# A hybrid decoder step: gate weights divided at another place of the state-space chunk, and zeroes of the expert buffer written in another stage

## The reference, cut to what matters

```
u = xn @ w_in
q, k, v, z, xbc, dt_raw, g_a, g_s = jnp.split(u, offs, axis=-1)
...
y_ssd, new_conv, new_ssm = _ssd_branch(z, xbc, dt_raw, ...)      # a scan over chunks of 128 tokens
merged = (jax.nn.sigmoid(g_a + b_gate[0]) * (y_attn @ w_attn_br)
          + jax.nn.sigmoid(g_s + b_gate[1]) * (y_ssd @ w_ssd_br))
h = x + merged @ w_out
...
h = h + _hier_moe(hn, ...)      # 32 experts, two per token
```

## Time and profile before

| what | number |
|---|---|
| median of 3 runs | 2184.7 us (2180.73 to 2187.69) |
| the profiled execution | 2187.37 us |
| its span | 2185.5 us |
| PE busy | 1899.6 us (87%) |
| DVE busy | 1201.7 us (55%) |
| ACT busy | 818.8 us (37%) |
| POOL busy | 390.8 us (18%) |
| DMA moved | 472.97 MB, mean 216 GB/s |
| prompt state space | about 850 to 1100 us of the span |
| merge | about 1166 to 1340 us of the span |

### The profile page before, as it was taken

The page is one execution under the profiler, slowest core; times in us unless marked ns, Lnnn a source line. Parts: engine busy times, 40 slices in busy tenths (PEclk is TensorE's granted clock), DMA queues, the critical chain, the costliest instruction groups (busy, mean ns, idle before and its releaser), DMA issues. The chain is left out here.

```text
span 2185.5 us, 29251 instructions
## 1 busy us (share of the span) xinstructions
PE 1899.6 (87%) x11737; PEld 1686.6 (77%) x11737; DVE 1201.7 (55%) x1224; ACT 818.8 (37%) x1173; POOL 390.8 (18%) x377
## 2 busy tenths in 40 slices
PE   7999999979986998888883897994899999999970
PEld 7899999978885987777652897883788888888850
DVE  5244443235654221555643554426888888888856
ACT  5211111123341321222232321213677777777732
POOL 0000000055523302011240000001831111111103
PEclk9999999989986999999986998996999999999985
DMA  6355555444427866233229434325999999999957
GB/s 227 128 166 166 166 166 166 143 148 138 127 81 190 212 169 201 92 114 104 80 70 321 141 104 133 128 85 207 351 420 407 407 406 402 402 408 406 401 211 261
DMA packets 203113, 472.97 MB, mean 216 GB/s; under 512 B 34519, under 2 KB 160887, under 8 KB 189922
## 3 DMA queue, kind: packets, MB, share of 16 engines
q1 hardware_dynamic: 134946, 319.29, 41.2%
q10 hardware_dynamic: 51440, 78.21, 9.8%
q0 software_dynamic: 16592, 73.60, 9.8%
HBM read 376.12 MB, written 121.93 MB: 228 GB/s over the span
## 5 line engine op out<-in xcount | busy, mean ns | idle before, releaser
L2736 DVE TENSOR_TENSOR k_w_lo<-expert_raw,k_w_hi 128x4096 fp32r<-128x4096 f32 x96 | 424.2, 4421 | 70.9 <-ACT k_w_hi L2680 70.9
L2680 ACT CAST k_w_hi<-expert_raw 128x4096 fp32r<-128x4096 f32 x96 | 348.4, 3633 | 107.2 <-PE k_pu L74 66.1
L72 PE MATMUL a_acc<-a_w_hi,x_hi 128*128 128x256 f32 x648 | 186.2, 287 | 0.3 <-DVE x_lo L229 0.3
L73 PE MATMUL a_acc<-a_w_lo,x_hi 128*128 128x256 f32 x648 | 184.3, 284 | 0.0
L74 PE MATMUL a_acc<-a_w_hi,x_lo 128*128 128x256 f32 x648 | 184.3, 284 | 0.0
L72 PEld LDWEIGHTS a_acc<-a_w_hi,x_hi 128*128 128x128 f32 x648 | 125.3, 193 | 0.7 <-DVE x_lo L229 0.5
L73 PEld LDWEIGHTS a_acc<-a_w_lo,x_hi 128*128 128x128 f32 x648 | 125.3, 193 | 0.0
L74 PEld LDWEIGHTS a_acc<-a_w_hi,x_lo 128*128 128x128 f32 x648 | 125.2, 193 | 0.0
L72 PE MATMUL k_pu<-k_w_hi,k_x_hi 128*128 128x512 f32 x256 | 105.0, 410 | 9.0 <-DVE k_w_lo L2736 9.0
L72 PE MATMUL k_po<-k_w_hi,k_h_hi 128*128 128x512 f32 x256 | 102.5, 400 | 10.6 <-DVE k_h_lo L2757 10.6
L72 PE MATMUL k_pg<-k_w_hi,k_x_hi 128*128 128x512 f32 x256 | 102.0, 399 | 2.7 <-DVE k_x_lo L2741 2.7
(11 more groups left out here) (458 smaller groups left out, 4853.3 us busy)
## 6 DMA issues: line engine op xcount, KB each, us to landing
expert_raw<-in_w_expert_gate SPq DMA_DIRECT2D x32, 2048.0 KB, 10.7
expert_raw<-in_w_expert_up SPq DMA_DIRECT2D x32, 2048.0 KB, 12.2
expert_raw<-in_w_expert_down SPq DMA_DIRECT2D x32, 2048.0 KB, 11.7
h<-in_cache_kv_w SPq DMA_DIRECT2D x72, 256.0 KB, 4.2
scratch_o_moe<-k_out ACTq DMA_DIRECT2D x32, 512.0 KB, 11.4
a_w<-in_w_in SPq DMA_DIRECT2D x15, 1024.0 KB, 7.2
scratch_u_tm<-h ACTq DMA_DIRECT2D x81, 128.0 KB, 2.1
scratch_o_moe<-h_zeros POOLq DMA_DIRECT2D x2, 4096.0 KB, 29.7
```

The source lines that it names most:

```text
L72: nc.tensor.matmul(out, one_pass(a_hi), one_pass(b_hi), start=(i == 0), stop=False)
L73: nc.tensor.matmul(out, one_pass(a_hi), one_pass(b_lo), start=False, stop=False)
L2680: nc.scalar.copy(one_pass(w_hi[:, kind, :]), raw[:, c % NRAW, :]).then_inc(s_hi, 1)
L2736: nc.vector.tensor_tensor(one_pass(w_lo[:, kind, :]), raw[:, c % NRAW, :], w_hi[:, kind, :], ALU.subtract).then_inc(s_lo, 1)
```

## The change

The division of tile n + 2 moves from the end of chunk n to between the second and the third weighing of chunk n. The zeroes for the unused expert rows are no longer written in the merge (two DMAs of 4,096 KB from a tile of 512 columns) but in the prompt state space: a tile of 256 columns of zeroes is filled at its start, and in each of the eight chunks POOL issues one DMA, behind its gating, that writes half of the 16 row blocks in a quarter of the columns. At the end of the stage POOL waits for all eight.

```
@@ phase_ssd_prompt
+        zeros, s_zeros, s_unused = sb("zeros", [128, 256]), sm("zeros"), sm("unused")
...
                 nc.gpsimd.memset(whole[:, :], 1.0)
+                nc.gpsimd.memset(zeros[:, :], 0.0).then_inc(s_zeros, 1)
                 nc.gpsimd.memset(hT[:, :], 0.0)
...
                     if n > 0:
                         gate(n - 1)
+                    if n == 0:
+                        pool.wait_ge(s_zeros, 1)
+                    a, b = n % 4, n // 4
+                    pool.dma_start(T["o_moe"][(NE + 8 * b) * 128:(NE + 8 * b + 8) * 128, a * 256:(a + 1) * 256].rearrange(
+                        "(b p) c -> p b c", p=128), bc(zeros[:, :].unsqueeze(1), [128, NOVF // 2, 256])).then_inc(s_unused, 16)
                 gate(N - 1)
+                pool.wait_ge(s_unused, 16 * N)
                 pool.wait_ge(s_h0, 16 * NB)
...
                     for q in range(NQ):
                         weigh(n, q)
+                        if q == 1:
+                            gates.split(dve, n + 2)
                     state(n, 0)
...
                     dve.sem_inc(s_free, 1)
-                    gates.split(dve, n + 2)
@@ phase_merge
-        zeros = sb("zeros", [128, 512])
...
-        s_const, s_eps, s_zeros, s_unused = sm("const"), sm("eps"), sm("zeros"), sm("unused")
+        s_const, s_eps = sm("const"), sm("eps")
...
                 nc.gpsimd.memset(T["m_T"][:, :, REAL:], 0.0)
-                nc.gpsimd.memset(zeros[:, :], 0.0).then_inc(s_zeros, 1)
-                pool.wait_ge(s_zeros, 1)
-                for a in range(D // 512):
-                    pool.dma_start(T["o_moe"][NE * 128:, a * 512:(a + 1) * 512].rearrange("(b p) c -> p b c", p=128),
-                                   bc(zeros[:, :].unsqueeze(1), [128, NOVF, 512])).then_inc(s_unused, 16)
-                pool.wait_ge(s_unused, 16 * (D // 512))
```

## The result

The changed kernel takes 2155.53 us (median of 4 runs, 2152.91 to 2158.01) against 2185.2 for the kernel before, a ratio of 0.9861 with an interval of 0.9849 to 0.9874: 30 us less. The forecast was 2154.

| stretch | before, us | after, us | difference |
|---|---|---|---|
| start to prompt state space | 849.97 | 847.65 | -2.3 |
| prompt state space: start to chunk 1 | 47.94 | 48.19 | +0.3 |
| chunks 1 to 6 | 173.45 | 150.54 | -22.9 |
| chunk 7 and end | 28.92 | 30.68 | +1.8 |
| sample state space | 66.12 | 67.32 | +1.2 |

A forecast was written before the change was run, and what follows sets the result against it. PE's order was taken to set the state space's length, its idle time being what can be won. 20.8 + 11.2 = 32.0 us off 2187.37 gives 2155.4, or 2152.7 from the median; forecast 2154, range 2147 to 2167.

The forecast's parts named there:

- Part 1, the division: Prompt state space, chunks 1 to 6: six PE waits for gate weights go, gaining 20.8 us (bounds 17.2 and 20.8).
- The low clock: Chunks 1 to 6: PE's low-clock stretches follow its waits and go with them, 3.6 of the 20.8 us.
- C: Cast's start in chunk 4; inputs end by C + 6.2, division C + 9.6, weighings C + 11 to 12, cost 0.
- The rule weighed against it: DVE and POOL lock their shared ports per instruction; the division pays POOL's gating at most once, sum staying 2155.4 us.
- Chunk 0: Prompt state space, chunk 0: division of tile 2 costs 0, up to 2.5 us if zeroes slow its weights.
- Part 2, the merge: Merge's start: without 8.4 MB of zeroes there, the second rows land earlier, gaining 11.2 us (bounds 7 and 13).
- The 10.7 for the first megabyte of weights: Merge's start: weights ahead of the rows take 16.8 us to land, 6.1 alone, so 10.7 us go.
- The 1.2 for the rows: Merge's start: the rows' own transfer, sharing DMA engines with the zeroes, is halved, gaining some 1.2 us.
- DVE as the bound: Rival, prompt state space: DVE's outputs come 1.6 us late six times, 10 us, time 2165; chance 0.08.
- The merge's start bound elsewhere: Rival, merge: only the division's gain counts, time 2166.6 us; chance 0.06.
- POOL held in its issues: Rival, prompt state space: issues of zeroes over 21 us lengthen chunks; at 27 us each, time 2202; chance 0.03.
- Weights or rows that come no earlier: Rival, both stages: neither part does what it says, time 2181 to 2190 us; chance 0.03.

The follow-up runs named there:

- the kernel with waits of 0.75 to 1.14 us: The kernel before, with POOL's skip product held until the division is done: 2167.71 us, one run.
- the repeated division: The change with each division repeated in its place, twice (2157.28 us, ratio 0.9868) and four times (2190.67 us, ratio 1.0017 to the kernel before).
- the run with two divisions: The change with each division done twice in its place: 2157.28 us, ratio 0.9868 to the kernel before.
- the zeroes alone: The kernel before with only the zeroes moved and the division still at the end of the chunk: 2174.27 us, ratio 0.9933.

## Why the prediction was right

- **Part 1, the division.** The mechanism held at each step: six waits gone, the cast 0.69, DVE early enough. The sum was 20.8 and the stage gave 20.9, but by two errors that cancel. The step "a chunk at clock 1.00 with its wait taken out is 27.90 - 2.47 = 25.4" was too long: the chunks take 25.1 (150.54 / 6), so chunks 1 to 6 gave 22.9. Of the 2.1 us between, 0.5 come from the window of 27.90 us, which is 0.09 wider than chunk 6 (27.81). The other 1.6 are six times 0.26 us by which that chunk, at clock 1.00, was longer than its wait of 2.47 and the 25.08 of the same chunk now; where they went was not found. Chunk 7, which I left out of the sum, took 1.8 back in this execution; the repeated runs show that it varies by 3 without the change's help.
- **The low clock** was a consequence of the waits, as taken: in the change and each version of it in which PE is not held longer than 0.5 us in chunks 1 to 6, and in the kernel with waits of 0.75 to 1.14 us, these chunks have 1.00; in the one with all of them, 0.97.
- **What hides the division.** I had the inputs ending by C + 6.2, the division by C + 9.6 and the last weighing by C + 11 to 12. In chunk 4, where C now is 971.18, they end at C + 4.2, C + 7.6 and C + 9.7: POOL's gating came late enough to meet neither the second input product, which takes 1.22 us and not the 2.86 of chunk 7, nor the cast. The state update starts at C + 11.1 and the output at C + 14.4, both still waiting for PE, where C + 11.3 and C + 14.6 were worked out. The room of 4.1 us behind it is measured by the repeated division.
- **The rule weighed against it** (the Trainium skill, SBUF — State Buffer, section "SBUF: two separate sides", the exclusive lock): the runs agree. With POOL's product moved away the cast takes 0.69 us where it took 2.34; beside the division POOL's gating takes 3.30 where it took 2.38; and a second cast behind the start of the gating takes 2.71, once, the next ones 0.69. POOL's issues of zeroes, on which the same section warns, took 0.92 us each, and 1.09 at most in any run; none was held longer.
- **Chunk 0.** The bound of 0 to 2.5 us, with 0 taken, for weights slowed by the first megabyte of zeroes: it was 0.66.
- **Part 2, the merge.** 11.2 was worked out, 11.4 measured; 9.7 to 11.9 us in each kernel that only keeps the zeroes from the merge's start, wherever it puts them, and 1.2 to 1.5 in the two that do not. The mechanism held, but the terms were not all sound, and that their sum comes so near is partly luck. The 10.7 for the first megabyte of weights was 9.6 (16.8 to 7.2 us), since tile 0's rows go ahead of it in both kernels; the prediction took off 0.7 for them and showed no row for it. The 1.2 for the rows does not follow from the pace it names (512 KB at 6.1 us a megabyte take 3.0); measured, the second rows came 10.8 us earlier, 1.2 more than the weights. PE's first product came 10.8 earlier too.
- **The rivals.** DVE as the bound: excluded by the run with two divisions. The merge's start bound elsewhere: excluded by the zeroes alone. POOL held in its issues: 0.92 us, not 21. Weights or rows that come no earlier: each part alone shows its own gain.

## What to carry to other kernels

A producer's step that stands at the end of a loop body can wait for the next body's first instructions on another engine. Look for a place in the middle where its inputs are long there and the engine waits anyway, and add up the waits behind that place: their sum is the room, and in the one chunk looked at here it held to a tenth of a microsecond. Bulk writes that nobody reads for long belong where the DMA engines are idle; at the start of a stage they stand in line with the loads that the stage begins with, and issued 48 us later in the same stage they did not lengthen it.

## What the runs showed of the hardware that was not expected

- A wait of PE of 2.4 to 4.5 us was followed by the lower clock (0.50) in some of the chunks 1 to 6, one of 0.75 to 1.14 us in none of them; the price of a removed wait can therefore be more than its length: 12.0 us of waits less gave 16.4 us, in one run. In chunk 7 a wait of 1.63 us was followed by the low clock in one kernel, and one of 2.76 was not in another.
- The same instructions of chunk 7 took 27.25 and 30.63 us in two kernels, by the moment at which the clock falls and rises again.
- POOL's copy of 16 columns, 0.2 us alone, takes 1.19 behind DVE's input product (0.66 before).
